# Scores for both query kinds from one product of 128 columns in the second layer's recurrence

## What is computed

```python
def step(s, inp):
    r_t, lw_t, k_t, v_t, kk_t, a_t = inp
    s_kk = jnp.einsum('bhik,bhk->bhi', s, kk_t)
    s = (s * jnp.exp(lw_t)[:, :, None, :]
         - s_kk[..., :, None] * (kk_t * a_t)[..., None, :]
         + v_t[..., :, None] * k_t[..., None, :])
    return s, jnp.einsum('bhij,bhj->bhi', s, r_t)
```

## Time and profile before

| | us |
|---|---|
| median of 3 runs | 1906.67 |
| lowest and highest | 1904.36 and 1910.46 |
| profiled execution | 1911.56 |
| its span in the trace | 1909.8 |
| recurrence, first `aT` to the last prompt unit's state | 1088.10 to about 1282.5 |
| av of unit 0, A inside units 0 and 6 | 1119.60, 1130.28, 1260.71 |

### The profile page before, as it was taken

One profiled execution on the slowest core, in us unless ns is written; L12 is line 12 of the kernel. 1 busy time (PEld: TensorE's weight loads), 2 busy tenths in 40 slices (PEclk: granted clock), 3 DMA queues, 4 the chain that ended last, 5 costly groups with the idle time before them and its releaser, 6 DMA issues.

```text
span 1909.8 us, 43023 instructions
## 1 busy us (share of the span) xinstructions
PE 1761.2 (92%) x18617; PEld 1665.2 (87%) x18617; DVE 981.6 (51%) x1407; ACT 725.0 (38%) x953; POOL 217.8 (11%) x307
## 2 busy tenths in 40 slices
PE   7999879799999999997999877779899999999997
PEld 6999876799999999997888767765599999999997
DVE  4487775644433444456788544433644442444444
ACT  4353444354522222333466223223445531222243
POOL 1042551000000000120060111112100000000000
PEclk8999989899999999998999878886799999999999
DMA  4321131332332333330222200010143232233321
GB/s 130 82 74 47 55 102 52 89 111 88 92 96 66 88 88 102 88 89 23 79 67 74 73 3 4 4 49 1 32 107 113 86 108 78 68 88 101 88 67 58
DMA packets 234669, 138.95 MB, mean 73 GB/s; under 512 B 4720, under 2 KB 229360, under 8 KB 234528
## 3 DMA queue, kind: packets, MB, share of 16 engines
q1 hardware_dynamic: 226784, 116.73, 21.2%
q0 software_dynamic: 4864, 15.90, 3.3%
q10 hardware_dynamic: 2880, 4.21, 0.6%
HBM read 128.66 MB, written 8.16 MB: 72 GB/s over the span
## 4 chain that ended last, share of the span: by engine, by line
PE 80%; DVE 9%; ACT 4%; issue 3%; POOL 2%; DMA 1%; ACTq 0%; SPq 0%; DVEq 0%; POOLq 0%
PE ps L351 62%; PE ps L1881 2%; PE ps L2505 1%; PE ps L1628 1%; ACT w_head L315 1%; DVE w_rest L320 1%; PE ps L2462 1%; PE ps L1862 1%; PE ps L2803 1%; POOL mix L984 1%; PE ps L1093 1%; PE ps L1169 1%; PE ps L2809 1%; PE ps L1900 1%; PE ps L3004 1%
## 5 line engine op out<-in xcount | busy, mean ns | idle before, releaser
L351 PE MATMUL ps<-x_split,w_head 128*128 128x272 f32 (+1 forms) x5312 | 900.0, 292 | 24.7 <-DVE x_split L1418 8.6
L351 PEld LDWEIGHTS ps<-x_split,w_head 128*128 128x128 f32 x5312 | 763.6, 191 | 38.5 <-issue 27.7
L351 PE MATMUL ps<-x_split,w_rest 128*128 128x272 f32 (+1 forms) x2656 | 555.5, 291 | 0.0
L315 ACT ACTIVATE w_head<-w_raw 128x1024 fp32r<-128x1024 f32 (+1 forms) x205 | 227.1, 1108 | 584.1 <-PE ps L351 566.8
L351 PEld LDWEIGHTS ps<-x_split,w_rest 128*128 128x128 f32 x2656 | 421.4, 191 | 0.0
L320 DVE TENSOR_TENSOR w_rest<-w_raw,w_head 128x1024 fp32r<-128x1024 f32 (+1 forms) x205 | 268.0, 1307 | 171.3 <-ACT w_head L315 171.2
L351 PE MATMUL ps<-hidden_split,w_head 128*128 128x272 f32 x1408 | 233.1, 287 | 0.0
L351 PEld LDWEIGHTS ps<-hidden_split,w_head 128*128 128x128 f32 x1408 | 198.0, 188 | 0.0
L351 PE MATMUL ps<-hidden_split,w_rest 128*128 128x272 f32 x704 | 145.3, 287 | 0.0
L1459 DVE TENSOR_TENSOR hT<-hT,ps 128x544 f32<-128x544 f32 (+1 forms) x40 | 28.8, 721 | 161.1 <-PE ps L351 161.1
L351 PEld LDWEIGHTS ps<-hidden_split,w_rest 128*128 128x128 f32 x704 | 110.0, 188 | 0.0
(11 more groups left out here) (454 smaller groups left out, 2136.5 us busy)
## 6 DMA issues: line engine op xcount, KB each, us to landing
w_raw<-in_w_ffn_gate SPq DMA_DIRECT2D x44, 512.0 KB, 3.7
w_raw<-in_w_ffn_up SPq DMA_DIRECT2D x44, 512.0 KB, 3.7
w_raw<-in_w_ffn_down SPq DMA_DIRECT2D x32, 704.0 KB, 4.7
w_raw<-in_w_in_even SPq DMA_DIRECT2D x29, 512.0 KB, 3.7
w_raw<-in_w_ple_gate SPq DMA_DIRECT2D x16, 512.0 KB, 3.9
w_raw<-in_w_out_even SPq DMA_DIRECT2D x8, 512.0 KB, 4.0
w_raw<-in_rw_wr SPq DMA_DIRECT2D x8, 512.0 KB, 3.8
w_raw<-in_rw_wk SPq DMA_DIRECT2D x8, 512.0 KB, 3.9
```

The lines of the kernel that those rows point to most:

```text
L315: act.activation(wh[:, s, 0:kt * P], raw[:, s, 0:kt * P], ACT.Copy).then_inc(head_ok[s], 1)
L351: mm = pe.matmul(ps[:, 2 * s + h, 0:half.stop - half.start], w[:, s, k * P:(k + 1) * P], x[:, k, half], start=first and k == 0, stop=k == ...
```

## The change

Four edits.

1. `aT` and `A` become one function `scores`, whose products take both query kinds at once: 128 columns instead of 64. The part `O` is gone, since its two groups are the second halves of these. A group's output now fills both banks, so `made_scores(m, 0)` and `made_scores(m, 1)` read its halves.
2. VectorE makes the masked r scores (`out_scores`) in two products of 64 partitions at `aT` (behind the transpose) and two at `A`. P2 has to wait for those at `aT`, since it writes over them. `sOs` gets a third buffer.
3. ScalarE copies all of U, in two operations of 64 partitions; VectorE's copy is gone, but for the sample unit.
4. A stream has 14 parts instead of 15, `HEAD` is 7 and the slots are dealt out anew.

```diff
-        sOs = [quad[:, 4096:5120], quad[:, 5632:6656]]
+        sOs = [ap.rearrange("p (c x) -> p c x", c=2)[:, :, 0:512] for ap in (
+            quad[:, 4096:5120], quad[:, 5632:6656], mix[:, 25600:28672])]
...
-            parts += [("A", 0), ("O", 0), ("vt", 0), ("kt", 0)]
+            parts += [("A", 0), ("vt", 0), ("kt", 0)]
...
-        HEAD = 8
+        HEAD = 7
...
-            order = ("o", "n", "o", "on", "n", "on", "nononon")[slot]
+            order = ("on", "", "o", "on", "on", "on", "nonon")[slot]
...
+            def scores(pe, b, bank):
+                for i, p, c in tile_heads:
+                    out = bank(1 - c)[half(p ^ b), i * 2 * CP:(i + 1) * 2 * CP].rearrange("p (s t) -> p s t", s=2)
+                    mm = pe.matmul(out, keys_p(2 * i + p, b)[half(c), m, :], qrF[half(c), 2 * i + p, :, tokens], start=True,
+                                   stop=True)
+                return mm
...
-                    for i, p, c in tile_heads:
-                        mm = pe.matmul(bank(1 - c)[half(1 - p), i * CP:(i + 1) * CP], keys_p(2 * i + p, 1)[half(c), m, :],
-                                       qrF[half(c), 2 * i + p, 0, tokens], start=True, stop=True)
+                    mm = scores(pe, 1, bank)
...
                         pe.wait_ge(*O2.act.at(f"aT{m}_0"))
                         pe.wait_ge(*O2.dve.at(f"t{m}_2"))
+                        pe.wait_ge(*O2.dve.at(f"O{m}_1"))
...
-                elif kind == "O":
-                    for b in range(2):
-                        for i, p, c in tile_heads:
-                            mm = pe.matmul(bank(c)[half(p ^ b), (2 * i + p) * CP:(2 * i + p + 1) * CP],
-                                           keys_p(2 * i + p, b)[half(c), m, :], qrF[half(c), 2 * i + p, 1, tokens], start=True,
-                                           stop=True)
+                    mm = scores(pe, 0, bank)
...
+        def out_scores(dve, m, b):
+
+            for p in range(2):
+                r = half(p ^ b)
+                mm = dve.tensor_tensor(sOs[m % 3][r].rearrange("p c (i b t) -> p c i b t", i=4, b=2)[:, :, :, p, :],
+                                       made_scores(m, 1)[r], scP[r, 1, :].unsqueeze(1).unsqueeze(1).to_broadcast([64, 2, 4, CP]),
+                                       ALU.mult)
+            return mm
...
             dve.transpose(xxs[m % 2], first).then_inc(*O2.dve.done(f"t{m}_2"))
+            dve.wait_ge(*O2.act.at(f"aT{m}_0"))
+            if m > 2:
+                dve.wait_ge(*O2.pe.at(f"o{m - 3}"))
+            out_scores(dve, m, 1).then_inc(*O2.dve.done(f"O{m}_1"))
...
+                        out_scores(dve, m, 0).then_inc(*O2.dve.done(name))
-                    elif kind == "O":
-                        for c in range(2):
-                            mm = dve.tensor_tensor(sOs[par][:, 512 * c:512 * c + 512].rearrange("p (n t) -> p n t", n=8),
...
-            dst = vus[n % 2][half(0), :, 1] if n < SAMPLE else vu_sample[32:64]
+            for p in range(2 if n < SAMPLE else 1):
+                dst = vus[n % 2][half(p), :, 1 - p] if n < SAMPLE else vu_sample[32:64]
...
-            dve.wait_ge(*O2.pe.at(f"U{n}"))
-            dst = vus[n % 2][half(1), :, 0] if n < SAMPLE else vu_sample[96:128]
+            if n == SAMPLE:
+                dve.wait_ge(*O2.pe.at(f"U{n}"))
```

More of the change, by code:

```diff
@@ L2466, in pe_stream @@
                 elif kind == "A":
-                    for i, p, c in tile_heads:
-                        mm = pe.matmul(bank(c)[half(p), i * CP:(i + 1) * CP], keys_p(2 * i + p, 0)[half(c), m, :],
-                                       qrF[half(c), 2 * i + p, 0, tokens], start=True, stop=True)
-                elif kind == "O":
-                    for b in range(2):
-                        for i, p, c in tile_heads:
-                            mm = pe.matmul(bank(c)[half(p ^ b), (2 * i + p) * CP:(2 * i + p + 1) * CP],
-                                           keys_p(2 * i + p, b)[half(c), m, :], qrF[half(c), 2 * i + p, 1, tokens], start=True,
-                                           stop=True)
+                    mm = scores(pe, 0, bank)
                 elif kind == "vt":
@@ L2549, in both, with made_scores @@
             return ps[:, bank_of(m, 0):bank_of(m, 0) + 2, 0:wide]
+        def made_scores(m, s):
+            return both(m, 512).rearrange("p c (i s t) -> p c i s t", i=4, s=2)[:, :, :, s, :]
+        def out_scores(dve, m, b):
[5 more added lines that the diff above has]
+            return mm
         def act_stream(act, m):
@@ L2578, in act_stream @@
                     else:
-                        dst = aTs[par].rearrange("p (c x) -> p c x", c=2)
-                        src = both(m, 256)
+                        dst, src = aTs[par].rearrange("p (c i t) -> p c i t", c=2, i=4), made_scores(m, 0)
                     act.activation(dst, src, ACT.Copy).then_inc(*O2.act.done(name))
@@ L2767, in pe_chunk @@
             for i, p, c in tile_heads:
-                mm = pe.matmul(ps[half(1 - p ^ c), 2 + c, i * NC:(i + 1) * NC], sA[half(p), head_cols(c, i)],
+                mm = pe.matmul(ps[half(1 - p ^ c), 2 + c, i * NC:(i + 1) * NC], sA[half(p), swap_cols(c, i)],
                                vu[half(p), i, p, c ^ p, :], start=i == 0, stop=n == 0, skip_group_check=True)
@@ L2803, in pe_chunk @@
                 pe.matmul(ps[half(g), 4 + p, 256 + i * CP:256 + (i + 1) * CP], vu[:, i, p, g, :],
-                          sO[:, 512 * c + (2 * i + p) * CP:512 * c + (2 * i + p + 1) * CP], start=n == 0 and i == 0, stop=True,
+                          sO[:, 1 - c, (2 * i + p) * CP:(2 * i + p + 1) * CP], start=n == 0 and i == 0, stop=True,
                           skip_group_check=True)
@@ L2859, in act_chunk @@
             act.wait_ge(*O2.pe.at(f"U{n}"))
-            dst = vus[n % 2][half(0), :, 1] if n < SAMPLE else vu_sample[32:64]
-            src = ps[half(0) if n < SAMPLE else slice(32, 64), 2:4, 256:512].rearrange("p g (i v) -> p g i v", i=4)
-            act.activation(dst.rearrange("p i g v -> p g i v"), src, ACT.Copy).then_inc(*O2.act.done(f"U{n}"))
+            for p in range(2 if n < SAMPLE else 1):
+                dst = vus[n % 2][half(p), :, 1 - p] if n < SAMPLE else vu_sample[32:64]
+                src = ps[half(p) if n < SAMPLE else slice(32, 64), 2:4, 256:512].rearrange("p g (i v) -> p g i v", i=4)
+                mm = act.activation(dst.rearrange("p i g v -> p g i v"), src, ACT.Copy)
+            mm.then_inc(*O2.act.done(f"U{n}"))
             go_on(3)
@@ L2877, in dve_chunk @@
             go_on(2)
-            dve.wait_ge(*O2.pe.at(f"U{n}"))
-            dst = vus[n % 2][half(1), :, 0] if n < SAMPLE else vu_sample[96:128]
-            src = ps[half(1) if n < SAMPLE else slice(96, 128), 2:4, 256:512].rearrange("p g (i v) -> p g i v", i=4)
-            dve.tensor_copy(dst.rearrange("p i g v -> p g i v"), src).then_inc(*O2.dve.done(f"U{n}"))
+            if n == SAMPLE:
+                dve.wait_ge(*O2.pe.at(f"U{n}"))
+                src = ps[96:128, 2:4, 256:512].rearrange("p g (i v) -> p g i v", i=4)
+                dve.tensor_copy(vu_sample[96:128].rearrange("p i g v -> p g i v"), src).then_inc(*O2.dve.done(f"U{n}"))
             go_on(3)
```

15 lines of the change are left out of this document (4 added, 11 removed).

## The result

| | before | changed |
|---|---|---|
| median, us (15 runs each) | 1905.67 | 1912.46 |
| lowest and highest | 1896.74 and 1931.52 | 1907.91 and 1935.44 |
| profiled execution | 1911.56 | 1910.03 |
| its span | 1909.8 | 1908.2 |

The ratio of the changed kernel to the kernel before is **1.0051, 95% interval 1.003 to 1.0072**, that is 5.7 to 13.7 us slower, 9.7 us at its middle; the medians above lie 6.8 us apart. The forecast was 4.6 us faster.

The account below looks back on a forecast made before the run. The prediction took TensorE's order and waits, for other engines and for instruction blocks, to bound the kernel. Start +3.0, six units -5.4 and end -2.2 gave -4.6 us, from 1906.67 to 1902 us, range 1893 to 1914.

Parts of the forecast that it names:

- The start: From the first aT to the first av, wider groups and VectorE's added products cost +3.0 us together.
- The wide group: On TensorE, a score group of 128 columns takes about 0.95 us from start to start.
- The wait before X3: TensorE idles 2.6 us for VectorE's factor of P3; A to X3 takes 4.2 us.
- Blocks of 256 instructions: TensorE's issue gaps are waits for its next 256 instructions, a block costing 3.85 and 4.16 us.
- Both together: Waits and instruction blocks combined in a recurrence unit: gain 0.5 to 1.6 us at full clock, 0.9 chosen, -5.4 for six.
- the walk through the waits: A unit at full clock without instruction waits: 17.2 us before, 17.75 changed, so the change costs 0.55 us.
- 2.0 us for a unit where blocks decide: Saving 64 matrix and 64 weight records, half a block, gains 2.0 us in a unit; otherwise 0.
- harmless as a sum (VectorE is half idle): VectorE's net +0.6 us in a unit does no harm as a sum, though two products precede P3's factor.
- The end: In unit 7, st7 behind sO gives -2.0 us, and an earlier first load 0.2 more.
- The waits alone: Rival: only waits count, +3.3 us for six units, +4.1 with the ends, 1911 us; chance 0.15.
- the clock: Rival: idleness before X3 brings half clock behind it in every unit, +7.4 us, 1914; chance 0.15.
- blocks decide throughout: Rival: the 2.0 us of saved instructions come in each of six units, -11.2 us, 1895.5; chance 0.17.

Follow-up runs that it names:

- after_warm: Changed kernel with two products of 512 columns added ahead of P3, their results written over: 1909.75 us, ratio 1.005 to the kernel before.
- after_narrow: Changed kernel with each wide score group made of 32 narrow products instead of 16 wide ones: 1921.46 us, ratio 1.0084 to the kernel before.
- after_tiny: Changed kernel with 16 more products of 4 columns ahead of P3 in units 2 to 7, results written over: 1911.12 us, ratio 1.0034.
- after_late: Changed kernel with VectorE's two r products at A moved behind the two operations on the state: 1914.09 us, ratio 1.0065 to the kernel before.
- after_one128: Changed kernel with VectorE's two r products at aT and two at A each made one of 128 partitions, misplacing some r scores: 1902.93 us, ratio 0.9989.
- after_no: Changed kernel with slot 5's two parts exchanged, so one stream's P3, transpose and factor precede the other's A: 1908.25 us, ratio 1.0012.

## Why the prediction was wrong

**What held.** The start: +2.6 us for +3.0. The first `aT` to P2 of stream 1, which answers to the earlier trace rows, took 11.05 us for the forecast 10.7:

```profile
1085.64 1.98 PE L2448 MATMUL ps<-mix 64*64 64x128 f32 x32 [2.78 <-DVE mix L2326]
1090.72 1.08 PE L2470 MATMUL ps<-odd_quad 64*64 64x32 f32 x32 [3.10 <-DVE odd_quad L2558]
...
1096.69 0.50 PE L2470 MATMUL ps<-odd_quad 64*64 64x32 f32 x21 [2.39 <-DVE odd_quad L2558]
```

The wide group: 0.92 us from start to start for 0.95. The half-height products: 0.69 each, as one of 128 partitions. The wait before X3: 2.87 for 2.6, A to X3 4.41 for 4.2. Blocks of 256 instructions: 28 packets for 3548 matrix and 3544 weight records in six units, 253 apart; from the issue gap at 1186.72 to that at 1190.75 there are 3+32+64+28 = 127 matrix records; and the issue gaps fell by half.

**The step that failed** is the one headed "Both together": "The gain is 0.5 to 1.6 us at full clock", and with it -0.9 us for a unit, -5.4 for six. The profiles have +3.0 us for the six, which by themselves they can't tell from none; but of the 9.7 us of the runs (5.7 at the least) the start holds only 2.6, so the rest got longer and not shorter. The step failed in two terms.

First, the walk through the waits was made at full clock, and put A to av at 8.75 us before and 8.05 after, a gain of 0.7 in that stretch. Measured, as means over the twelve units of two profiles, it is 10.2 before and 10.7 after, a loss of 0.5. Most of that loss is the sixth unit's, where state products stand ahead of av: 11.7 us before and 13.5 after. In the other five it is 9.9 before and 10.1 after, so what failed there is that the gain of 0.7 didn't come. The wait itself was priced rightly; what was left out is that the chain behind it, X3, vt, P4, kt, X4 and av, runs wholly or in part at half clock: 5.5 us in the mean of those units, instead of the 4.2 of `after_warm`, where the walk had 3.85. That the clock there costs time in the whole isn't shown, since `after_warm` was no faster. I had put that into a rival that "decides once the mean clock of the units is 0.80 or less". The mean was 0.87 and 0.79 in the two profiles (0.87 and 0.95 before), but the mean is not what counts: with 0.87 as with 0.79 the half clock fell on part of the stretch where each group is waited for, on kt in every unit. The other stretch, av to A, came out at 11.1 before and 11.2 after, where the walk had 8.45 and 9.7: a loss of 1.25 forecast for it didn't come either.

Second, the "2.0 us for a unit where blocks decide" were too dear. The instructions of two narrow groups are worth some 0.8 us in the changed kernel (`after_narrow`). As I read it, a new long wait for VectorE lies in the unit and TensorE's instructions arrive meanwhile (`after_tiny`: free there). I had seen that "the long gap before X3 can't be shared fully with the blocks"; the gap is the price of the change, and by this reading it swallows the gain of the change.

The call that VectorE's net +0.6 us is "harmless as a sum (VectorE is half idle)" is where the engine's share misled. In its place it is 11 us: one operation of 0.68 us out of that queue takes the ratio from 1.0051 to 0.9993, and only changing the places of P3 and A to 1.0012. Moving the pair alone behind the factor (`after_late`, 1.0065) gave nothing, as TensorE waits for the pair too.

**The end** was forecast at -2.2 us and came out at +0.6 for the stretch from av6 on. This term too was mis-sized, and rows 9 show it: st7 had waited 0.40 us, so sO ahead of it could fill 0.40 at the most, and not 2.0. St7 does stand behind sO now, which answers to the earlier trace rows:

```profile
1264.86 0.71 PE L2487 MATMUL ps<-ident,mix 64*128 64x64 f32 x8 [0.60 <-ACT mix L2592]
...
1270.09 0.68 PE L2487 MATMUL ps<-ident,mix 64*128 64x64 f32 x8 [2.23 <-DMA mix<-in_state_rwkv]
...
1275.07 1.09 PE L2487 MATMUL ps<-ident,mix 64*128 64x64 f32 x8 [0.99 <-DMA mix<-in_state_rwkv]
1276.09 1.97 PE L2809 MATMUL ps<-odd_quad 128*64 128x64 f32 x32
1277.99 1.11 PE L2487 MATMUL ps<-ident,mix 64*128 64x64 f32 x8
```

But the first state product is not earlier by 0.2: it begins 6.1 us after A of unit 6 (1258.74) instead of 4.5, so its buffer is free for the next load that much later, and TensorE then waits 2.23 and 0.99 us for DMAs, where it was 0.94, 0.91 and 0.40. In the second pair of profiles it begins 5.6 us after A instead of 4.5, and those waits are 2.7 us in all instead of 2.3. The order moved as forecast; what the loads depend on moved the other way.

**The rivals.** The waits alone gave 1911 us and the clock 1914; the measured 1912.46 lies between. That the waits' +0.55 us for a unit is near the +0.5 of the profiles is luck: it was -0.7 from A to av and +1.25 from av to A, and measured are +0.5 and +0.1. That blocks decide throughout is refuted. The two rivals were taken as alternatives; the traces show their signs together, the half clock behind the wait and fewer issue gaps beside it. How the loss divides between them isn't shown.

**Open.** Why A to av gained in `after_one128`, `after_warm` and `after_no` (9.5, 9.3 and 8.9 us), while av to A lost part of it again (11.7, 11.8 and 12.3), isn't settled; in `after_no` part of this is only that A stands a group later. Of the 9.7 us in the ratio the two pairs of profiles show 6.2 in the recurrence; the rest lies within what single profiles vary. Edit 3's worth inside the changed kernel (0.13%) is not resolved.

## What to carry to other kernels

Read an added operation by what stands behind it in its engine's queue, not by the engine's share: VectorE was half idle, and 0.7 us in its queue ahead of the factor cost more than all else. Where the added operation is waited for itself, moving it behind its neighbour doesn't help (`after_late`); putting the whole of the neighbour's work ahead did (`after_no`). When two sorts of cost run beside each other (a fetch, a wait), first ask whether the change's new wait covers the very gap that it was to save. And where a wait on the path grows beyond the others, look at the clock that the trace shows behind such gaps, and not at the unit's mean; but before paying for a higher one, test it, since here it gave no time.

## What the runs showed of the hardware

- A product over 64 partitions and 512 elements out of the banks takes VectorE 0.69 us, as over 128; one of 128 partitions 0.68. The Trainium skill, "VectorE: DVE Perf Modes", section "Why `tensor_reduce` can't reduce along partition axis", says that data stream along the free dimension through a pipeline for each partition, and the trace agrees.
- 32 records of 64 rows take 0.49 us from start to start at full clock for 32 or 64 columns, and 0.92 for 128: two query kinds at once save instructions, but next to no matrix time.
- With an idle stretch of 2.1 to 2.9 us ahead of X3, kt, the third group behind X3, ran at half clock in all of twelve units (1.85 to 1.97 us), while X3 and vt did so in some and not in others (X3 took 0.67 to 1.08 us). With two long products in that stretch and 0.8 us left idle, kt ran at full clock (1.09 us) in four of six. This alone changed no time that could be measured (1.005 beside 1.0051).
- An instruction's price depends on where it stands: 16 products of 4 columns in each of six units cost 3.4 us in one kernel (0.6 to 6.3) and nothing that the runs show in the other.
